# Two heads at a time on halves of the array, and the softmax's reciprocals in the transposing product, in the attention of two latent blocks

## The reference, cut to what matters

```
s_loc = einsum(q, k) * scale            # + window mask
s_ctx = einsum(q, kc) * scale
p = softmax(concat([s_loc, s_ctx, sink]))
attn = p_loc @ v + p_ctx @ vc
mix = concat([attn, fourier_mix(u, w_fourier)]) @ w_out
```

## Time and profile before

| | |
|---|---|
| median of 3 runs | 3018.24 us (3010.39 to 3019.68) |
| the profiled execution | 2997.13 us, its span 2995.3 us |
| PE busy | 1797.1 us, 60% of the span |
| DVE busy | 1871.4 us, 62% |
| ACT busy | 341.8 us, 11% |
| mean granted TensorE clock | 0.768 of 2.4 GHz |
| attention of `l0` (first score to first `w_out` product) | 59.86 us |
| attention of `l1` | 59.91 us |

### The profile page before, as it was taken

One profiled execution on the slowest core, in us unless ns is written; L12 is line 12 of the kernel. 1 busy time (PEld: TensorE's weight loads), 2 busy tenths in 40 slices (PEclk: granted clock), 3 DMA queues, 4 the chain that ended last, 5 costly groups with the idle time before them and its releaser, 6 DMA issues.

```text
span 2995.3 us, 23021 instructions
## 1 busy us (share of the span) xinstructions
PE 1797.1 (60%) x7921; PEld 1312.6 (44%) x7921; DVE 1871.4 (62%) x3359; ACT 341.8 (11%) x738; POOL 1051.9 (35%) x1045
## 2 busy tenths in 40 slices
PE   7889444185352234131326077892188999987998
PEld 5668111175141124021215066641157786476873
DVE  1435999878769886989987989558944200243001
ACT  1311101121001110001101000000013100021000
POOL 1002444577356665445765445336700000000000
PEclk9979656587575567565667589895588999988999
DMA  7357999999999999698999789999960554512443
GB/s 241 109 190 261 399 397 401 332 378 357 358 400 408 406 399 402 247 339 328 397 400 402 281 314 389 370 368 401 372 225 8 189 155 146 193 43 72 153 155 112
DMA packets 361764, 860.83 MB, mean 287 GB/s; under 512 B 23720, under 2 KB 148912, under 8 KB 361520
## 3 DMA queue, kind: packets, MB, share of 16 engines
q0 software_dynamic: 148000, 537.07, 46.5%
q1 hardware_dynamic: 213648, 322.29, 31.1%
HBM read 858.23 MB, written 1.05 MB: 287 GB/s over the span
## 4 chain that ended last, share of the span: by engine, by line
PE 36%; DMA 24%; DVE 18%; issue 15%; POOL 4%; ACT 2%; DVEq 0%; SPq 0%; ACTq 0%
PE bank L842 12%; DMA RING<-in_peer_v,EX 8%; PE bank L856 8%; PE bank L375 7%; DMA RING<-in_peer_u,EX 5%; DMA W<-in_ada_w 3%; DMA WORK<-in_peer_v,EX 3%; DVE ACC L1514 3%; POOL RING L951 2%; DMA W<-in_w_up 2%; PE bank L363 2%; PE bank L384 2%; POOL WORK L951 1%; DVE hrows L1529 1%; DMA WORK<-in_peer_u,EX 1%
## 5 line engine op out<-in xcount | busy, mean ns | idle before, releaser
L951 POOL DMA_INDIRECT RING<-in_peer_u,EX x343 | 323.5, 943 | 580.9 <-DVE EX L1490 300.2
L842 PE MATMUL bank<-HT,W 128*128 128x256 f32 x2112 | 476.6, 389 | 43.3 <-DMA W<-in_w_up 17.6
L842 PEld LDWEIGHTS bank<-HT,W 128*128 128x128 f32 x2112 | 411.8, 196 | 108.0 <-DMA W<-in_w_up 19.6
L951 POOL DMA_INDIRECT RING<-in_peer_v,EX x341 | 373.9, 1096 | 236.7 <-DVE hrows L1529 121.5
L1514 DVE SCALAR_TENSOR_TENSOR ACC<-RING,hrows 128x1024 bf16<-128x1024 f32 x343 | 402.9, 1217 | 48.6 <-DMA RING<-in_peer_u,EX 40.2
L363 PE MATMUL bank<-consts,XN 128*128 128x128 f32 x224 | 47.0, 390 | 469.8 <-DVE XN L1358 229.6
L407 PE MATMUL bank<-W,CACT 128*32 128x512 f32 x768 | 164.0, 957 | 268.3 <-DMA W<-in_ada_w 117.8
L375 PE MATMUL bank<-W,HT 128*128 128x256 f32 (+1 forms) x1120 | 245.9, 382 | 14.1 <-ACT HT L1003 7.3
L363 PEld LDWEIGHTS bank<-consts,XN 128*128 128x128 f32 x224 | 40.6, 207 | 475.6 <-DVE XN L1358 232.2
L1529 DVE SCALAR_TENSOR_TENSOR ACC<-RING,ACTS,ACC 128x1024 f32<-128x1024 f32 x168 | 215.4, 1282 | 46.2 <-DMA RING<-in_peer_v,EX 46.1
L1529 DVE SCALAR_TENSOR_TENSOR hrows<-RING,ACTS,hrows 128x1024 f32<-128x1024 f32 x168 | 216.2, 1287 | 43.0 <-DMA RING<-in_peer_v,EX 42.6
(11 more groups left out here) (323 smaller groups left out, 2259.6 us busy)
## 6 DMA issues: line engine op xcount, KB each, us to landing
W<-in_ada_w SPq DMA_DIRECT2D x48, 1024.0 KB, 13.4
W<-in_w_ada SPq DMA_DIRECT2D x48, 1024.0 KB, 14.0
W<-in_w_in SPq DMA_DIRECT2D x35, 1024.0 KB, 9.3
W<-in_w_gate SPq DMA_DIRECT2D x33, 1024.0 KB, 5.7
W<-in_w_up SPq DMA_DIRECT2D x33, 1024.0 KB, 5.5
W<-in_w_down SPq DMA_DIRECT2D x33, 1024.0 KB, 5.0
W<-in_peer_wq SPq DMA_DIRECT2D x24, 1024.0 KB, 16.7
W<-in_w_o SPq DMA_DIRECT2D x12, 1024.0 KB, 14.3
```

The costliest lines, as they stand in the source:

```text
L842: mm = pe.matmul(bs[j][:, g * S:(g + 1) * S], w[:, k, j * P:(j + 1) * P], HT[:, k, :], start=(k == 0 and g == 0), stop=(k == DC - 1 and g ...
L951: gp.indirect_dma_start(SLOT[g % NS], None, rows, bass.IndirectOffsetOnAxis(EX[:, t, k:k + 1], 0))\
```

## The change

It applies to latent blocks only; in the context block the code is laid out anew and the exponential of the sink is taken in two halves ahead of the scores' instead of once behind them. In the latent blocks:

- Score products take 64 partitions: head `e` of a pair uses rows `64e` to `64e + 63` of the array, and its partner the other rows. The two go to different banks.
- Both tiles' scores are issued ahead of any probabilities. Tile 1's stand in the gather ring's memory (`RING`), which is idle by then.
- ScalarE scales and copies the context half of each score bank (mark `sx`), VectorE the latent half, and VectorE frees the bank.
- The transposes become ordinary products with a diagonal matrix of the reciprocals (`DG`, four heads at a time, made by VectorE, mark `dg`), so what comes out is transposed and already divided.
- In the value products the operands change places: values are loaded (64 columns), the probabilities stream, and head `e` of a pair writes partitions `64e` to `64e + 63` of `OB`, that is columns `64e` on of the array. The output is already transposed; a plain copy brings it to `HT` (mark `oe`), and `cT`, its copies and the multiplication by reciprocals go.

```
+SL = (S2_["l"], RING[:, 0:4, :].rearrange("p s n -> p (s n)").rearrange("p (h n) -> p h n", h=H2))
+DG = RING[:, 4, :].rearrange("p (e h n) -> p e h n", e=2, h=4)
...
+if who == "l":
+    rows = [slice(e * HD, (e + 1) * HD) for e in range(2)]
+    for t in range(NT):
+        for c in range(H2 // 2):
+            bs = [open_bank(("s", p, t, 2 * c + e), V) for e in range(2)]
+            for i, keys_ in enumerate((KTL, (KC0, KC1)[l])):
+                mms = [pe.matmul(bs[e][:, i * S:(i + 1) * S], QT2[rows[e], c, t * P:(t + 1) * P],
+                                 keys_[rows[e], 2 * (c // 2) + e, :], start=True, stop=True) for e in range(2)]
+            mms[0].then_inc(filled, 1)
+            mms[1].then_inc(filled, 1)
+    for t in range(NT):
+        if t == 1:
+            pe.wait_ge(mark("oe", p), 1)
...
+        def values(c):
+            wait_empty(pe, ("pT", p, t, 2 * c), ("pT", p, t, 2 * c + 1))
+            g = slice((c // 2) * HD, (c // 2 + 1) * HD)
+            for k in range(4):
+                vals = QKV[:, k, 640:768][:, g] if k < 2 else (VC0, VC1)[l][:, k % 2, g]
+                for e in range(2):
+                    mm_ = pe.matmul(OB[rows[e], c * P:(c + 1) * P], vals, PT2[:, (2 * c + e) % 4, k, :],
+                                    start=(k == 0), stop=(k == 3))
+            return mm_
+        for h in range(H2):
+            pe.wait_ge(mark("dg", p), 2 * t + h // 4 + 1)
+            b = open_bank(("pT", p, t, h), VA[h % 2])
+            for k in range(4):
+                mm = pe.matmul(b[:, k * P:(k + 1) * P], SL[t][:, h, k * P:(k + 1) * P], DG[:, h // 4, h % 4, :],
+                               start=True, stop=True)
             mm.then_inc(filled, 1)
+            if h % 2 and h > 1:
+                values(h // 2 - 1)
+        values(H2 // 2 - 1).then_inc(mark("o", p), 1)
+    pe.wait_ge(mark("oe", p), 2)
...
+def exponentials(t, S2, half):
+    hs = slice(half * (H2 // 2), (half + 1) * (H2 // 2))
+    act.wait_ge(mark("smax", p), 2 * t + half + 1)
+    do(A(SE[:, t, hs], SE[:, t, hs], ACT.Exp), mark("se", p))
+    for h in range(hs.start, hs.stop):
+        do(A(S2[:, h, :], S2[:, h, :], ACT.Exp, bias=MX8[:, t, h:h + 1], accum_out=SUM8[:, t, h:h + 1]),
+           mark("ex", p))
...
+def context_scores(t, heads):
+    for h in heads:
+        b = wait_full(act, ("s", p, t, h))
+        do(A(SL[t][:, h, S:2 * S], b[:, S:2 * S], ACT.Copy, scale=HD ** -0.5), mark("sx", p))
...
+else:
+    context_scores(0, range(H2))
+    fourier()
+    for half in range(2):
+        exponentials(0, SL[0], half)
+        context_scores(1, range(4 * half, 4 * half + 4))
+    for half in range(2):
+        exponentials(1, SL[1], half)
+        probabilities(0, (4 * half + 1, 4 * half + 3))
+    probabilities(1, range(1, H2, 2))
+for i in halves if both else ():
...
+else:
+    def scores(t, half):
+        hs = half_heads[half]
+        for h in range(hs.start, hs.stop):
             b = wait_full(ve, ("s", p, t, h))
-            do(ve.scalar_tensor_tensor(out=S2[:, h, 0:S], in0=b[:, 0:S], scalar=HD ** -0.5, in1=win[:, t, :],
-                                       op0=ALU.mult, op1=ALU.add))
-            free(("s", p, t, h), ve.tensor_scalar(S2[:, h, S:2 * S], b[:, S:2 * S], HD ** -0.5, None, ALU.mult))
+            ve.wait_ge(mark("sx", p), t * H2 + h + 1)
+            free(("s", p, t, h), ve.scalar_tensor_tensor(out=SL[t][:, h, 0:S], in0=b[:, 0:S], scalar=HD ** -0.5,
+                                                         in1=win[:, t, :], op0=ALU.mult, op1=ALU.add))
...
+    def diagonals(t, half):
+        hs = half_heads[half]
+        if t:
+            wait_full(ve, ("pT", p, 0, 4 * half + 3))
+        ve.wait_ge(mark("ex", p), t * H2 + 4 * half + 4)
+        inverse_sums(t, hs)
+        do(ve.tensor_tensor(DG[:, half, :, :], ident.unsqueeze(1).to_broadcast([P, 4, P]),
+                            RS8[:, t, hs].unsqueeze(2).to_broadcast([P, 4, P]), ALU.mult), mark("dg", p))
...
+    def values(t):
+        ve.wait_ge(mark("o", p), t + 1)
+        do(ve.tensor_copy(HT[:, 0:4, t * P:(t + 1) * P], OB[:, :].rearrange("p (c n) -> p c n", c=4)), mark("oe", p))
+    scores(0, 0)
+    scores(0, 1)
+    scores(1, 0)
+    diagonals(0, 0)
+    diagonals(0, 1)
+    scores(1, 1)
+    for half in range(2):
+        probabilities(0, (4 * half, 4 * half + 2))
+        diagonals(1, half)
+    values(0)
+    probabilities(1, range(0, H2, 2))
+    values(1)
```

More of the change, by code:

```diff
@@ L822, in block2 @@
                     if j == 0:
-                        wait_empty(pe, ("cT", p, 0), ("cT", p, 1), ("fo", p, 0), ("fo", p, 1))
+                        wait_empty(pe, ("fo", p, 0), ("fo", p, 1), *[("cT", p, i) for i in range(2) if who == "c"])
                     by_tokens(("mx", p, j), V, w, 256, HT)
@@ L1226, in block2 @@
                         copy(("mw", p, i), MW[:, 2 * i:2 * i + 2, :, :], lambda b: b[:, :].rearrange("p (c e n) -> p c e n", c=2, e=2))
-                for t in range(NT):
-                    if both:
+                def exponentials(t, S2, half):
[5 more added lines that the diff above has]
+                           mark("ex", p))
@@ new lines, in context_scores, with fourier, probabilities @@
+                def context_scores(t, heads):
+                    for h in heads:
+                        b = wait_full(act, ("s", p, t, h))
+                        do(A(SL[t][:, h, S:2 * S], b[:, S:2 * S], ACT.Copy, scale=HD ** -0.5), mark("sx", p))
+                def fourier():
+                    for i in range(2):
+                        copy(("fo", p, i), HT[:, 4 + 2 * i:6 + 2 * i, :], lambda b: two(b[:, :]))
+                def probabilities(t, heads):
+                    for h in heads:
+                        copy(("pT", p, t, h), PT2[:, h % 4, :, :],
+                             lambda b: b[:, 0:nb * P].rearrange("p (b n) -> p b n", b=nb))
@@ L1229, in block2 @@
+                if both:
+                    for t in range(NT):
                         for h in range(H2):
                             copy(("s", p, t, h), S2[:, h, :], lambda b: b[:, 0:S], scale=HD ** -0.5)
-                    if t == 0:
-                        for i in range(2):
-                            copy(("fo", p, i), HT[:, 4 + 2 * i:6 + 2 * i, :], lambda b: two(b[:, :]))
-                    for h in range(H2):
-                        if h % (H2 // 2) == 0:
-                            act.wait_ge(mark("smax", p), 2 * t + h // (H2 // 2) + 1)
-                        do(A(S2[:, h, :], S2[:, h, :], ACT.Exp, bias=MX8[:, t, h:h + 1], accum_out=SUM8[:, t, h:h + 1]),
-                           mark("ex", p))
@@ L1239, in block2 @@
-                    do(A(SE[:, t, :], SE[:, t, :], ACT.Exp), mark("se", p))
-                    for h in range(H2) if both else range(1, H2, 2):
-                        copy(("pT", p, t, h), PT2[:, h % 4, :, :],
-                             lambda b: b[:, 0:nb * P].rearrange("p (b n) -> p b n", b=nb))
-                for i in halves:
+                        if t == 0:
+                            fourier()
+                        for half in range(2):
+                            exponentials(t, S2, half)
@@ new lines, in block2 @@
+                        probabilities(t, range(H2))
+                else:
+                    context_scores(0, range(H2))
+                    fourier()
+                    for half in range(2):
[5 more added lines that the diff above has]
+                    probabilities(1, range(1, H2, 2))
@@ L1995, in block2 @@
-                    yield
-                    for h in range(0, H2, 2) if who == "l" else ():
-                        copy(("pT", p, t, h), PT2[:, h % 4, :, :],
-                             lambda b: b[:, 0:nb * P].rearrange("p (b n) -> p b n", b=nb))
-                    ve.wait_ge(mark("se", p), t + 1)
-                    do(ve.tensor_tensor(RS8[:, t, :], SUM8[:, t, :], SE[:, t, :], ALU.add))
-                    settle()
-                    do(ve.reciprocal(RS8[:, t, :], RS8[:, t, :]))
@@ L2009, in block2 @@
+                    scores(0, 1)
[3 more added lines that the diff above has]
+                    scores(1, 1)
+                    for half in range(2):
+                        probabilities(0, (4 * half, 4 * half + 2))
[3 more added lines that the diff above has]
+                    values(1)
                 if who == "l":
-                    copy(("cT", p, 0), HT[:, 0:2, :], lambda b: two(b[:, :]))
```

123 lines of the change are left out of this document (64 added, 59 removed).

## The result

The kernel after takes 2973.62 us (median of 4 runs, 2971.76 to 2976.77), the kernel before, with a fourth run beside the three, 3014.31 (3004.35 to 3019.68): ratio 0.987, 95% interval 0.9839 to 0.99. The forecast was 2994 with a range of 2981 to 3010, so the gain, 40.7 us between the medians, came out larger than forecast (24.4). The profiled executions differ by less: spans of 2995.3 and 2970.3, 25.0 us apart. All medians in this document leave out the one slow run there was, 3149.70 us at a granted clock of 0.695, an execution of before beside the runs f1 to f4.

A forecast was written before the change was run, and what follows sets the result against it. In the attention PE was taken to bound where busy, and between, twice, a chain of maxima and exponentials. A block gains 12.2 us, both 24.4, so 3018.24 - 24.4 = 2994 us, range 2981 to 3010.

The forecast's parts named there:

- VectorE's third half: VectorE's pass over tile 1's first score half, starting 13.6 us into a block after idling 3.3 us for ScalarE's context copies.
- the first diagonal product: PE's first probabilities of a latent block, forecast 19.0 us in, after sums, reciprocal and diagonal; before: 13.45.
- the first values: Tile 0's first value products, forecast 24.9 us into the block, after VectorE's fourth half and its copies of probabilities.
- tile 1: Tile 1's probabilities and values on PE, forecast to start 34.8 us into the block and take 11.0 us.
- My own working: Step-by-step timing of a latent block: 46.8 us, plus 0.9 missed on the old order, 47.7; 12.2 gained a block.
- A change of shape: Switch of PE's array shape in the latent blocks, taken as 0.12 us each from a 0.09 reading at `ada`.
- 13 us on end: PE clock in a latent block, forecast at 0.50 from 14 to 27 us in, after PE idles from 10.05.
- the 5.30 us: Stretch of the old block around tile 1's maxima and exponentials, given with 1.35 us as PE waiting.
- most of the gain: Claim that the gain mostly comes from laying tile 1's maxima and exponentials beside tile 0's probabilities; 12.2 us a block altogether.
- Halves: Row and column halves run fully side by side: 0.86 us a pair for scores or values, instead of 1.72 or 1.71.
- The context block: One more small exponential (0.2 us) a tile there, hidden under DMA: nothing; 0.4 us if that cover were gone.
- The step that failed: Carrying the attention's 24.4 us gain unchanged to the whole kernel: 2972.7 us for a profile, 2994 for the median.

The follow-up runs named there:

- f1: Kernel after with exponentials transposed undivided and the reciprocals multiplied in at the output (late division): 2957.70 us, ratio 0.9859, block 42.01.
- f4: Kernel after with a pair's value products in twos, two of one head, then two of the other: 2965.79 us, ratio 0.988, block 46.86.
- e3: Kernel after in its order and score-copy split alone, without halves or diagonals: 2995.62 us, ratio 0.9965, rest 730.2.
- c2: Kernel before with only the context block's part of the change (sink's exponential in two halves): 3005.18 us, ratio 0.9994.
- c1: Kernel before, unchanged, as a control: 3008.70 us, ratio 1.0016.
- c3: Kernel after with the context block as it was before, so the latent blocks' part alone: 2971.79 us, ratio 0.9893.
- c4: Kernel after, unchanged, timed beside the controls: 2976.91 us, ratio 0.9902.
- e1: Kernel after with score products back on all 128 rows: 2983.99 us, ratio 0.9931, rest 720.9.
- e2: Kernel after with a pair's value products as four of one head, then four of the other: 2980.59 us, ratio 0.9908, block 49.68.
- e4: Kernel after with the values of two pairs issued together after every four heads' probabilities: 2979.03 us, ratio 0.9911, block 45.85.
- f2: Kernel after with the late division, Fourier steps moved, two pairs' values together and reciprocals spread earlier: 2953.45 us, ratio 0.9834.
- f3: Kernel after, unchanged, once more: 2965.11 us, ratio 0.988.
- g1: Kernel before with only the score products of the latent blocks on row halves: 3012.49 us, ratio 1.0039, rest 764.5.
- g2: Kernel after with scores on all rows and a pair's values head by head: 2976.56 us, ratio 0.9933, block 51.57.
- g3: Kernel after, unchanged, a fourth time: 2964.97 us, ratio 0.9897, block 46.67, rest 717.1.

## Why the prediction was wrong

**The attention: right, its terms near.** VectorE's third half starts 13.9 us into the block (13.6 forecast), behind ScalarE's copies as said; the first diagonal product at 19.3 (19.0); the first values at 25.2 (24.9); tile 1 at 34.0 (34.8); the end at 46.55. My own working had 46.8 and I then added 0.9, because the same working had missed the old block by that much: 47.7, 1.1 too long a block, 2.2 to 2.3 for both. The 46.8 was close partly by luck. A change of shape costs 0.22 on the mean, not 0.12, some 1.1 us a block on the path. Against it, the clock was low for 6.9 us in `l0` (2 x 0.19 x 9.17 + 2 x 0.29 x 5.91), with a return between, and back at 24.3 us, where I had 13 us on end, until 27. In `l1` it was low for 10.2 us (0.89 over 46.55), and the block is as long. Small slips of the working don't matter to this: 4 x 0.33 + 0.11 + 2.8 is 4.23 and not 4.25, 12 x 0.86 + 5 x 0.12 is 10.9 and not 11.0, and of the 5.30 us that it gives as PE waiting PE waited for 4.01. That the hidden chain is "most of the gain" was wrong: the order alone is half (e3).

**Halves: right.** A pair's score products take 0.87 us, 0.97 with the change of shape ahead, and a pair's 16 value records 0.87. The Trainium skill, TensorE: Matmul & The Clock Gate (Measured speedup vs the span model), gives 2.38 for three column tiles; two column halves here reach the full 2. The Trainium skill, TensorEngine Tiling (Array Packing), Key Properties, says that a change of the tiling mode drains the engine; the trace agrees that a change costs time, 0.27 and 0.17 us.

**The context block: right** (c2, nothing).

**The step that failed** is the last: "The attention has no DMA, so the difference carries over as it is: 2997.1 - 24.4 = 2972.7 for a profile, 3018.24 - 24.4 = 2994 for the median." For the profile that held to 0.6 us (2972.12), partly by luck: the rest gave 2.2 us more than the 24.4, and the profile of after happened to reach `l0`'s first score product 1.6 us later than that of before (2253.15, 2251.56). For the median it put the change on top of three runs, as if their median were the program's. What each group measured ahead of `l0`'s first score product, medians in us:

| group | before | the others |
|---|---|---|
| forecast's 3 runs | 2272.7 | |
| result | 2268.8 (4 runs) | after 2254.7 |
| c | 2262.7 (23 runs) | c1 2263.0, c2 2259.5, c3 2253.0, c4 2258.0 |
| e | 2262.1 (22) | e1 2261.3, e2 2255.4, e3 2263.6, e4 2260.0 |
| f | 2255.4 (10) | f1 2245.8, f2 2245.5, f3 (after) 2246.3, f4 2243.7 |
| g | 2254.5 (18) | g1 2246.2, g2 2247.2, g3 (after) 2246.1 |

The stage that gathers moves by itself: 2248.9 to 2281.5 in the 23 runs of before in group c alone. In the profiles the difference grows along the stage and has no one place: a table load of ScalarE (`ACT_TABLE_LOAD`) comes at 1526.07 us in c2 and at 1510.24 in f4, a later one at 1954.04 and 1932.48, and the first score product at 2266.37 and 2240.71. The median of the forecast's three runs lay 10 to 18 us above the group medians of the 73 runs of before that followed. Of the 40.7 us, then, 26.6 lie from `l0`'s first score product on, where the two attentions are, and 14.1 ahead of it (2268.8 less 2254.7). Of the 20.2 us by which the forecast was off, 2.2 are the attention (26.6 against 24.4) and 18.0 lie ahead of it (2272.7 less 2254.7). I had the sign of this before me: the profiled run lay 21.1 below the median, with nothing in it that explained 21 us, and I used that as an offset and not as the width of the base. I took 9 us, the spread of three runs, where the 23 runs spread by 33.

**What stays open.** Not all of the 14 is shown to be a draw. In the groups c, f and g the kernel after lies 4.7, 9.1 and 8.4 us below before in that stage. So do c3 (9.7), f1 (9.6), f2 (9.9), f4 (11.7), g1 (8.3) and g2 (7.3), while c1 (before itself), c2, e1, e3 and e4 lie within 3.3 and e2 6.7 below. My theory of a draw by the stage alone misses g1, g2 and g3, the rival of after's order and buffers misses g1, and that of row halves misses g2, which has none. The lowest runs are alike (group g: before 2239.1, g1 2236.8, g2 2238.3, g3 2243.5); what the low programs lack is runs far above (g: before up to 2275.6, g3 up to 2254.7). The profiles start that product between 2240.71 (f4) and 2266.37 (c2); none caught a run above that. So the medians of after and before are 31 to 41 us apart, of which the traces explain 26.6. Whether the remainder would hold for another build wasn't tried.

## What to carry to other kernels

Forecast a difference from the traces, but the time from a base whose spread is known: with three runs of a program whose largest stage waits for gathers, the range must hold where that base can lie, whatever the change does. Where two products can share the array, they need not stand right beside each other: here two places did, four products of one half in a row did not. Packing is worth as much as leaving work out: with the row halves and half of the column overlap undone (g2) a block is 5.0 us longer, with the doubled transposes and the wait for the diagonals gone (the late division) 4.5 shorter. Moving work beside other work is worth as much again (the order alone, 6.7).

## What the runs showed of the hardware that was not expected

- A product on a free column half may overtake: it started together with a product of the other half that stands two places ahead of it in the program (e2 at 2292.25 and 2292.26; f4, 46.86 us a block).
- A change of array shape: 0.27 us into column halves, 0.17 out of them.
- With score products on half the lanes in the old order, the clock stayed at or near 1.2 GHz through stretches of 17.94 and 27.80 us of other products behind them (g1: 0.53, then 0.52 and 0.50), and the kernel was slower (ratio 1.0039); with the same halves in the new order it wasn't (after: 0.93 over the block).
- The same stage, with the same instructions and load, took 7.29 and 8.68 us with the clock granted in it (0.85, 0.64): a gain can be given back far behind the place of the edit, here in the next block's first stage.
